# The last 512 output columns of each feed-forward computed block by block of tokens

## The chip, the core and the metric

One Trainium2 core out of eight runs the whole program. The metric is device microseconds of one execution; the times shown are the median of several. All data is fp32, the batch is 1, there are 512 tokens of width 1024.

## The reference, cut to what matters

The program is a first block (an mLSTM and pooling mixer and a mixture of 32 experts) followed by a second one of two layers. The change lies in the two feed-forwards of the second block and in the last norm:

```python
def rms_norm_2(x, g):
    xf = x.astype(jnp.float32)
    y = xf * lax.rsqrt(jnp.mean(xf * xf, axis=-1, keepdims=True) + EPS)
    return (y * g.astype(jnp.float32)).astype(x.dtype)

def swiglu(h, w_gu, w_down):
    gu = h @ w_gu
    g, u = jnp.split(gu, 2, axis=-1)
    return (jax.nn.silu(g) * u) @ w_down

def second_block(x, ...):
    k = v = None
    for l in range(DEPTH_2):            # 2 layers
        if l < N_A:                     # layer 0: gmlp
            x = x + gmlp_mixer(rms_norm_2(x, a_norm[l]), ...)
        else:                           # layer 1: attention
            k, v = shared_kv(x, kv_norm, kv_w)
            x = x + diff_attention(rms_norm_2(x, b_norm[j]), k, v, ...)
        x = x + swiglu(rms_norm_2(x, ffn_norm[l]), ffn_w_gu[l], ffn_w_down[l])
    return rms_norm_2(x, final_norm)
```

The hidden width of a feed-forward is 2816, that is 22 slices of 128.

## The kernel before

**Products.** Every fp32 factor is held as two fp32r parts, high and low, and a product is three matmuls (`mm3`: high x high, high x low, low x high), 128x128 stationary and 512 columns moving. The token matrix X stands in SBUF as four blocks (`tb`) of 128 tokens.

**The stream of weights.** `Stream` (W) holds all weights in the order of their use as items of at most 1 MB. SyncE loads each into a raw buffer. ScalarE makes the high part (`W.high`, L191, or L195 where a gain is multiplied in), VectorE the low part (`W.low`, L210, or L214 with a gain), each in two halves. There are four places for pairs of high and low parts (two early on, three within attention, of which the first `vv` item keeps one). An item's place may be written once the item that stood there before is released: `W.ends[before]`, for which ScalarE waits in `W.high`. `W.depth(j)` says how many items from j on have a predecessor in their place that is older than j. `W.high(e, j + W.depth(j))` and `W.low(...)` split up to there.

**The banks of sums.** `Ring` (R) plans the eight PSUM banks ahead: `R.claim` waits until a bank is free, `R.fill` tells that it is full, `R.free` that it has been read.

**A feed-forward** (`ffn_pe`, `ffn_act`, `ffn_vec`) runs over three groups of slices, 8, 8 and 6. In each group gate and up products (`fg`, `fu`) give the hidden values AT, and then the down products `fd{l}.{f0}.{h}` give half h (512 columns) of the output for all four blocks of tokens. Each half takes two weight items, of 4 and 4 slices, in the last group of 4 and 2. `n_pe` runs over the items outside and over the blocks inside: all four blocks with the first item, then all four with the second. The first item is released in the middle (`W.mid`, semaphore `w_used`), the second by the last full bank. `nd` counts the down items of a layer, 0, 2, ... 10; `nd == 10` is the last half of the last group, `fd{l}.16.1`.

VectorE adds each bank to X (`add_vec`, L845). For `fd{l}.16.1` it also calls `then`: one block behind the add it waits for ScalarE's sum of squares (`rms_act`, L689) and GpSimd's root (`rms_pool`, L694 and L696), then scales the rows. After feed-forward 0 the scaling is `normalize_vec` (L706), and `late_features_pe(e, 3)` transposes the rows (L731) into eight banks, of which ScalarE and VectorE make `hT4h` and `hT4l` (L761, L769). Behind that attention's products begin. `late_features_pe` also issues an unused product (`idle_pe`) ahead of block 0 and another ahead of slices 4 to 6. After feed-forward 1 the scaling is `last`, the output's norm (L260, `X<-X,small,GF`), and ScalarE issues the stores of the rows (L3075, L3077), each one block late.

**The order around the change**, in each engine's own queue. ScalarE: `W.high` for both items of the pair, then squares of blocks 0 to 3. VectorE: `W.low` for both items, then adds and `then`. The items that follow the last pair of layer 0 are two of `vv` (v weights), then `q`, `k`, `q`, ... Nothing follows the last pair of layer 1.

Of the kernel before, what the change touches and what calls it, by code (L numbers as in the profile page):

```python
# [11 lines left out]
ALU = mybir.AluOpType  # L12
# [3 lines left out]
P = 128  # L16
D = 1024
T = 512
TB = 4
# [213 lines left out]
def program(nc, g, out):  # L233
    ctx = ExitStack()
    with ctx:
# [19 lines left out]
        S = Sems(nc, ctx)  # L255
        R = Ring(S, [ctx.enter_context(nc.psum_tensor(f"ps{i}", [P, 512], F32)) for i in range(8)])
        W = Stream(S)

        def stt(e, o, x, s, y, o1, o2):
            return e.scalar_tensor_tensor(out=o, in0=x, scalar=s, in1=y, op0=o1, op1=o2)  # L260

        def mm(e, o, l, r, start, stop):
            return e.matmul(o, l, r, start=start, stop=stop, skip_group_check=True)  # L263

        def mm3(e, o, l, r, start, stop):
            mm(e, o, l[0], r[0], start, False)
            mm(e, o, l[0], r[1], False, False)
            return mm(e, o, l[1], r[0], False, stop)


        X = sb("X", [P, TB, D])
# [6 lines left out]
        small = sb("small", [P, 64])  # L278
        LASTG = sb("LASTG", [P, 4])
        LASTI = sb("LASTI", [P, 4], I32)  # L280
        GF = sb("GF", [P, D])
# [109 lines left out]
        AT = [sb("ATh", [P, 8, T], F32R), sb("ATl", [P, 8, T], F32R)]  # L391
# [101 lines left out]
        def n_plan(name, item, js, freed):  # L493
            for j in js[:-1]:
                W.mid(j)
            R.plan(name, TB, freed)
            W.ends[js[-1]] = R.full(name, TB - 1)

        A_, V_ = "bank_act", "bank_vec"
# [104 lines left out]
        def ffn_plan(l):  # L604
            R.plan(f"tf{2 if l == 0 else 4}", 8, V_)
            ng = nd = 0
            for f0, fn in FG:
                for f in range(0, fn, 2):
                    R.plan(f"fg{l}.{ng}", 2, A_)
                    W.ends[W.index[f"fg{l}"][ng]] = R.full(f"fg{l}.{ng}", 1)  # L610
                    R.plan(f"fu{l}.{ng}", 2, V_)
                    W.ends[W.index[f"fu{l}"][ng]] = R.full(f"fu{l}.{ng}", 1)
                    ng += 1
                for h in range(2):
                    n_plan(f"fd{l}.{f0}.{h}", "fd", W.index[f"fd{l}"][nd:nd + 2], V_)
                    nd += 2

        ffn_plan(0)
# [101 lines left out]
        def idle_pe(e, b, n):  # L720

            for _ in range(n):
                mm(e, b[:, :].rearrange("p (a n) -> p a n", a=4), ident[:, :], ident[:, :].unsqueeze(1).broadcast_to([P, 4, P]),
                   True, True)

        def late_features_pe(e, c):

            def turn(tb, kcs):
                for kc in kcs:
                    b = R.bank(f"tf{c}", kc)  # L730
                    i = e.transpose(b[:, tb * P:(tb + 1) * P], XN[:, tb, kc * P:(kc + 1) * P], ident[:, :])  # L731
                    if tb == TB - 1:
                        i.then_inc(*R.fill(f"tf{c}", kc))

            for kc in range(4):
                R.claim(e, f"tf{c}", kc)
            def rows(tb):
                return S("xn"), SECOND[tb] if c == 1 else 4 * norm_of[c] + tb + 1

            for tb in range(3):  # L740
                e.wait_ge(*rows(tb))
                if tb == 0:
                    idle_pe(e, R.bank(f"tf{c}", 0), 1)
                turn(tb, range(4))
            for kc in range(4, 7):
                R.claim(e, f"tf{c}", kc)
            idle_pe(e, R.bank(f"tf{c}", 4), 1)
            for tb in range(3):
                turn(tb, range(4, 7))
            e.wait_ge(*rows(3))  # L750
            turn(3, range(7))
            R.claim(e, f"tf{c}", 7)
            for tb in range(TB):
                turn(tb, [7])
# [82 lines left out]
                seen += kn  # L837
                k0 = (k0 + kn) % nk

        def add_vec(e, names, h, then=None):  # L840

            hs = slice(h * 512, (h + 1) * 512)
            for tb, name in enumerate(names):
                e.wait_ge(*R.full(*name))
                e.tensor_tensor(X[:, tb, hs], X[:, tb, hs], R.bank(*name)[:, :], ALU.add).then_inc(*R.free(*name))  # L845
                if then is not None and tb > 0:
                    then(tb - 1)
            if then is not None:
                then(TB - 1)


# [1566 lines left out]
        def ffn_pe(e, l, hT, AT, c):  # L2418
            late_features_pe(e, c)
            ng = nd = 0  # L2420
            for f0, fn in FG:
                for f in range(0, fn, 2):
                    for m in ("fg", "fu"):
                        t_pe(e, W.index[f"{m}{l}"][ng], [(f"{m}{l}.{ng}", 0), (f"{m}{l}.{ng}", 1)], hT,
                             (lambda kc: feature(e, c, kc)) if ng == 0 and m == "fg" else None, True)
                    ng += 1
                for h in range(2):
                    n_pe(e, W.index[f"fd{l}"][nd:nd + 2], f"fd{l}.{f0}.{h}", AT, 0, fn,
                         (lambda kc: e.wait_ge(S("a_lo"), 22 * l + f0 + kc + 1)) if h == 0 else None)
                    nd += 2  # L2430

        def ffn_act(e, own, l, hT, AT, c, norm, x_ready):
# [27 lines left out]
        def ffn_vec(e, own, l, hT, AT, c, then):  # L2460
            features_vec(e, c, hT, lambda kc: col("fn", 8 * l + kc))
            ng = nd = 0
            for f0, fn in FG:
                for f in range(0, fn, 2):
                    for m in ("fg", "fu"):
                        j = W.index[f"{m}{l}"][ng]
                        W.low(e, j + W.depth(j))
                    for k in range(2):
                        e.wait_ge(*R.done(f"fg{l}.{ng}", k))
                        e.wait_ge(*R.full(f"fu{l}.{ng}", k))  # L2470
                        e.tensor_tensor(tmpT[k][:, :], tmpT[k][:, :], R.bank(f"fu{l}.{ng}", k)[:, :], ALU.mult).then_inc(  # L2471
                            *R.free(f"fu{l}.{ng}", k))
                        e.wait_ge(S("a_hi"), 22 * l + f0 + f + k + 1)
                        e.tensor_tensor(AT[1][:, f + k, :], tmpT[k][:, :], AT[0][:, f + k, :].bitcast(F32),
                                        ALU.subtract).then_inc(S("a_lo"), 1)
                    ng += 1
                for h in range(2):
                    for j in W.index[f"fd{l}"][nd:nd + 2]:
                        W.low(e, j + W.depth(j))
                    add_vec(e, [(f"fd{l}.{f0}.{h}", tb) for tb in range(TB)], h, then if f0 + fn == 22 and h == 1 else None)  # L2480
                    nd += 2


# [573 lines left out]
        @block.scalar  # L3057
        def _(e):
            own = Own(S("act_self"))
            first_act(e, own)  # L3060
            experts_act(e, own)
            more_act(e)
            join_act(e, own)
            gmlp_act(e, own)
            ffn_act(e, own, 0, hT3, AT, 2, 4, lambda tb: R.done("go1", tb))
            attn_act(e, own)
            e.wait_ge(*R.done("as7", 7))
            e.dma_start(GF[:, :], g["final_norm_2"].partition_broadcast(P)).then_inc(S("fgb"), 16)
            ffn_act(e, own, 1, hT5, AT5, 4, 6, lambda tb: R.done(f"ao1.{tb}"))
            for tb in range(TB):  # L3070
                e.wait_ge(*R.done("fd1.16.1", tb))
                rms_act(e, 7, tb)
                if tb > 0:
                    e.wait_ge(S("x_last"), tb)
                    e.dma_start(out[0, (tb - 1) * P:tb * P, :], X[:, tb - 1, :]).then_inc(S("out"), 16)  # L3075
            e.wait_ge(S("x_last"), 4)
            e.dma_start(out[0, 3 * P:, :], X[:, 3, :]).then_inc(S("out"), 16)  # L3077
            e.wait_ge(S("out"), 64)

        @block.vector  # L3080
        def _(e):
            own = Own(S("vec_self"))
            first_vec(e, own)
            experts_vec(e, own)
            more_vec(e)
            join_vec(e, own)
            gmlp_vec(e, own)
            ffn_vec(e, own, 0, hT3, AT, 2, lambda tb: normalize_vec(e, 5, tb))
            attn_vec(e, own)

            def last(tb):
                e.wait_ge(S("rstd"), 4 * 7 + tb + 1)
                if tb == 0:
                    e.wait_ge(S("fgb"), 16)
                stt(e, X[:, tb, :], X[:, tb, :], small[:, 8 + tb:9 + tb], GF[:, :], ALU.mult, ALU.mult).then_inc(S("x_last"), 1)

            ffn_vec(e, own, 1, hT5, AT5, 4, last)

# [41 lines left out]
```

## Time and profile before

| | |
|---|---|
| median of 3 runs | 2085.39 us (2083.49 to 2088.24) |
| profiled execution | 2085.79 us |
| its span | 2084.0 us |
| mean granted TensorE clock | 0.983 of 2.4 GHz |
| TensorE busy | 1966.2 us, 94% |
| VectorE busy | 1188.4 us, 57% |
| ScalarE busy | 970.2 us, 47% |
| GpSimd busy | 186.4 us, 9% |

Busy time of TensorE counts matmuls whose ends are modelled. In the timelines each row begins with its start and its length in us, both from the span's start; a row with x2 or more merges neighbours of one kind. Brackets give the idle time of the engine before the row and what ended it.

### The profile page before, as it was taken

Reading aid. Unit: us, or ns where it says so; the run is one execution under the profiler, and the core shown is the slowest. Engines: PE = TensorE matmul, PEld = TensorE weight load, DVE = VectorE, ACT = ScalarE, POOL = GpSimd, SP = SyncE. Lnnn points to the kernel's source line nnn. Section 1 sums busy time; section 2 is a strip of 40 time slices with the busy share of each in tenths; the row PEclk is TensorE's granted clock in tenths of the full one; section 3 lists DMA queues with packets and bytes.
Section 4 is the critical chain, followed back from the end, with each engine's and each line's share of the span. In section 5 each row is a group of like instructions: output and inputs, shape, how many; then the busy total and the mean of one; then the engine's idle time right before and its main releaser. Section 6 shows DMA issues by size and latency. Waiting matters only on the chain.

```text
span 2084.0 us, 22887 instructions
## 1 busy us (share of the span) xinstructions
PE 1966.2 (94%) x8924; PEld 1572.5 (75%) x8924; DVE 1188.4 (57%) x1547; ACT 970.2 (47%) x1469; POOL 186.4 (9%) x250
## 2 busy tenths in 40 slices
PE   4989989999999999989999999998999989999997
PEld 3758767777777777758888888886777768888886
DVE  7776688888888888862543333324345343333322
ACT  3433268778878787744232222124445442222221
POOL 3100110121211110010000000001011100000000
PEclk8999999999999999999999999999999999999999
DMA  8464479999999999952323323222112123323211
GB/s 282 158 210 168 172 245 337 352 352 368 357 351 349 345 335 349 331 174 81 101 81 101 102 81 101 91 91 84 61 41 81 41 68 125 101 98 101 87 39 41
DMA packets 199832, 366.49 MB, mean 176 GB/s; under 512 B 13450, under 2 KB 83863, under 8 KB 199722
## 3 DMA queue, kind: packets, MB, share of 16 engines
q1 hardware_dynamic: 180960, 342.91, 47.6%
q10 hardware_dynamic: 8714, 11.46, 1.6%
q0 software_dynamic: 10048, 10.62, 1.5%
q8 instruction: 73, 1.20, 0.2%
q14 instruction: 37, 0.30, 0.0%
HBM read 365.05 MB, written 24.65 MB: 187 GB/s over the span
## 4 chain that ended last, share of the span: by engine, by line
PE 87%; DVE 7%; DMA 2%; issue 2%; ACT 1%; SPq 1%; POOL 0%; DVEq 0%; POOLq 0%; ACTq 0%
PE ps L263 85%; DVE wlo L210 2%; DMA raw<-in_w_in 1%; PE ps L2031 1%; DVE GM L2104 1%; SPq L886 1%; PE ps L731 1%; DMA raw<-in_ada_w 0%; DMA raw<-in_w_expert_down 0%; DVE acc L260 0%; PE ps L2608 0%; DVE hT5l L260 0%; DVE hT4l L769 0%; DVE X L845 0%; ACT XN L689 0%
## 5 line engine op out<-in xcount | busy, mean ns | idle before, releaser
L210 DVE TENSOR_TENSOR wlo<-raw,whi 128x1024 fp32r<-128x1024 f32 (+1 forms) x576 | 671.5, 1216 | 317.2 <-ACT whi L191 313.7
L191 ACT ACTIVATE whi<-raw 128x1024 fp32r<-128x1024 f32 (+1 forms) x576 | 573.0, 1047 | 232.8 <-PE ps L263 215.2
L263 PE MATMUL ps<-hT5h,whi 128*128 128x512 f32 x352 | 137.8, 391 | 6.3 <-DVE wlo L210 6.3
L263 PE MATMUL ps<-hT5l,whi 128*128 128x512 f32 x352 | 137.5, 391 | 0.0
L263 PE MATMUL ps<-hT3h,whi 128*128 128x512 f32 x352 | 137.0, 389 | 0.6 <-DVE hT3l L260 0.6
L263 PE MATMUL ps<-hT5h,wlo 128*128 128x512 f32 x352 | 137.4, 390 | 0.0
L263 PE MATMUL ps<-hT3l,whi 128*128 128x512 f32 x352 | 136.9, 389 | 0.0
L263 PE MATMUL ps<-hT3h,wlo 128*128 128x512 f32 x352 | 136.9, 389 | 0.0
L2471 DVE TENSOR_TENSOR tmpT<-tmpT,ps 128x512 f32<-128x512 f32 x44 | 30.1, 684 | 139.6 <-PE ps L263 139.6
L263 PE MATMUL ps<-whi,XT1h 128*128 128x512 f32 x256 | 102.1, 399 | 0.0
L263 PE MATMUL ps<-whi,XT0h 128*128 128x512 f32 x256 | 101.0, 395 | 1.1 <-DVE XT0l L2057 1.1
L263 PE MATMUL ps<-whi,XT1l 128*128 128x512 f32 x256 | 100.6, 393 | 0.0
L263 PE MATMUL ps<-wlo,XT1h 128*128 128x512 f32 x256 | 100.4, 392 | 0.0
L263 PE MATMUL ps<-whi,XT0l 128*128 128x512 f32 x256 | 99.8, 390 | 0.0
L263 PE MATMUL ps<-whi,GTh 128*128 128x512 f32 x256 | 99.7, 389 | 0.0
L263 PE MATMUL ps<-wlo,XT0h 128*128 128x512 f32 x256 | 99.7, 389 | 0.0
L263 PE MATMUL ps<-wlo,GTh 128*128 128x512 f32 x256 | 99.6, 389 | 0.0
L263 PE MATMUL ps<-whi,GTl 128*128 128x512 f32 x256 | 99.6, 389 | 0.0
L845 DVE TENSOR_TENSOR X<-X,ps 128x512 f32<-128x512 f32 x64 | 43.3, 686 | 92.4 <-PE ps L263 92.4
L694 POOL TENSOR_SCALAR small<-small 128x1 f32<-128x1 f32 x32 | 11.0, 342 | 946.5 <-ACT XN L689 888.4
L2446 ACT ACTIVATE tmpT<-ps 128x512 f32<-128x512 f32 x44 | 26.4, 600 | 134.7 <-PE ps L263 132.9
L263 PEld LDWEIGHTS ps<-hT5h,whi 128*128 128x128 f32 x352 | 66.5, 189 | 20.4 <-issue 6.5
(446 smaller groups left out, 4062.5 us busy)
## 6 DMA issues: line engine op xcount, KB each, us to landing
raw<-in_w_expert_gate SPq DMA_DIRECT2D x64, 1024.0 KB, 8.2
raw<-in_w_expert_up SPq DMA_DIRECT2D x64, 1024.0 KB, 8.0
raw<-in_w_expert_down SPq DMA_DIRECT2D x64, 1024.0 KB, 6.7
raw<-in_ffn_w_gu SPq DMA_DIRECT2D x44, 1024.0 KB, 5.0
raw<-in_ffn_w_down SPq DMA_DIRECT2D x20, 1024.0 KB, 5.0
raw<-in_ada_w SPq DMA_DIRECT2D x24, 512.0 KB, 5.4
raw<-in_w_in SPq DMA_DIRECT2D x8, 1024.0 KB, 5.7
raw<-in_a_w_in SPq DMA_DIRECT2D x8, 1024.0 KB, 9.3
```

The costliest lines, as they stand in the source:

```text
L191: e.activation(hi[:, c], raw[:, c], ACT.Copy).then_inc(self.S("w_hi"), 1)
L210: e.tensor_tensor(lo[:, c], raw[:, c], hi[:, c].bitcast(F32), ALU.subtract).then_inc(self.S("w_lo"), 1)
L263: return e.matmul(o, l, r, start=start, stop=stop, skip_group_check=True)
L694: e.tensor_scalar(out_, x, EPS, None, ALU.add).then_inc(*own.up())
L731: i = e.transpose(b[:, tb * P:(tb + 1) * P], XN[:, tb, kc * P:(kc + 1) * P], ident[:, :])
L845: e.tensor_tensor(X[:, tb, hs], X[:, tb, hs], R.bank(*name)[:, :], ALU.add).then_inc(*R.free(*name))
L886: e.dma_start(EARLY[n].rearrange("p (c n) -> p c n", c=2), ada_w[:, 2 * c:2 * c + 2, j * D:(j + 1) * D]).then_inc(S(f"early{n}"), 16)
L2031: i = e.transpose(b[:, k * P:(k + 1) * P], GM[:, k * P:(k + 1) * P], ident[:, :])
L2104: e.tensor_tensor(GM[:, :], SG[n % 2][:, :], R.bank(f"eu{n}")[:, :], ALU.mult).then_inc(*R.free(f"eu{n}"))
L2446: e.activation(tmpT[k][:, :], R.bank(f"fg{l}.{ng}", k)[:, :], ACT.Silu).then_inc(*R.free(f"fg{l}.{ng}", k))
L2471: e.tensor_tensor(tmpT[k][:, :], tmpT[k][:, :], R.bank(f"fu{l}.{ng}", k)[:, :], ALU.mult).then_inc(*R.free(f"fu{l}.{ng}", k))
```

## The change

The last down half of each feed-forward (`nd == 10`) is computed by a new function `blocks_pe`, which has the blocks of tokens outside and both items inside. The middle release of the pair's first item is gone: both items are released by the last block's full bank. `add_vec` gets a parameter `apart`; with it `then(tb)` is called right behind add tb. The feed-forwards pass it, the other callers don't. The first unused product of `late_features_pe` is left out for attention (`c == 3`). The last block of output rows is scaled and stored in two halves of 512 columns, and the stores of the other blocks are issued right behind their own square.

```diff
@@ ffn_plan
                 for h in range(2):
-                    n_plan(f"fd{l}.{f0}.{h}", "fd", W.index[f"fd{l}"][nd:nd + 2], V_)
+                    js = W.index[f"fd{l}"][nd:nd + 2]
+                    if nd < 10:
+                        n_plan(f"fd{l}.{f0}.{h}", "fd", js, V_)
+                    else:
+
+                        R.plan(f"fd{l}.{f0}.{h}", TB, V_)
+                        for j in js:
+                            W.ends[j] = R.full(f"fd{l}.{f0}.{h}", TB - 1)
                     nd += 2
@@ late_features_pe
+        APART = (3,)
...
-                if tb == 0:
+                if tb == 0 and c not in APART:
                     idle_pe(e, R.bank(f"tf{c}", 0), 1)
@@
-        def add_vec(e, names, h, then=None):
+        def blocks_pe(e, js, name, hT):
+
+            for tb in range(TB):
+                b = R.claim(e, name, tb)
+                kc, nk = 0, sum(W.w[j][1] for j in js)
+                for j in js:
+                    kn = W.w[j][1]
+                    for k in range(kn):
+                        if tb == 0 and 2 * k % kn == 0:
+                            e.wait_ge(*W.half(j, 2 * k // kn))
+                        i = mm3(e, b[:, :], [x[:, kc, tb * P:(tb + 1) * P] for x in hT], [x[:, k, :] for x in W.parts(j)],
+                                kc == 0, kc == nk - 1)
+                        kc += 1
+                i.then_inc(*R.fill(name, tb))
+
+        def add_vec(e, names, h, then=None, apart=False):
...
-                if then is not None and tb > 0:
+                if then is not None and apart:
+                    then(tb)
+                elif then is not None and tb > 0:
                     then(tb - 1)
-            if then is not None:
+            if then is not None and not apart:
                 then(TB - 1)
@@ ffn_pe
-                    n_pe(e, W.index[f"fd{l}"][nd:nd + 2], f"fd{l}.{f0}.{h}", AT, 0, fn,
-                         (lambda kc: e.wait_ge(S("a_lo"), 22 * l + f0 + kc + 1)) if h == 0 else None)
+                    if nd < 10:
+                        n_pe(e, W.index[f"fd{l}"][nd:nd + 2], f"fd{l}.{f0}.{h}", AT, 0, fn,
+                             (lambda kc: e.wait_ge(S("a_lo"), 22 * l + f0 + kc + 1)) if h == 0 else None)
+                    else:
+                        blocks_pe(e, W.index[f"fd{l}"][nd:nd + 2], f"fd{l}.{f0}.{h}", AT)
@@ ffn_vec
-                    add_vec(e, [(f"fd{l}.{f0}.{h}", tb) for tb in range(TB)], h, then if f0 + fn == 22 and h == 1 else None)
+                    add_vec(e, [(f"fd{l}.{f0}.{h}", tb) for tb in range(TB)], h, then if f0 + fn == 22 and h == 1 else None, True)
@@ ScalarE, end
-                if tb > 0:
-                    e.wait_ge(S("x_last"), tb)
-                    e.dma_start(out[0, (tb - 1) * P:tb * P, :], X[:, tb - 1, :]).then_inc(S("out"), 16)
-            e.wait_ge(S("x_last"), 4)
-            e.dma_start(out[0, 3 * P:, :], X[:, 3, :]).then_inc(S("out"), 16)
-            e.wait_ge(S("out"), 64)
+                if tb < TB - 1:
+                    e.wait_ge(S("x_last"), tb + 1)
+                    e.dma_start(out[0, tb * P:(tb + 1) * P, :], X[:, tb, :]).then_inc(S("out"), 16)
+            for h in range(2):
+                e.wait_ge(S("x_last"), TB + h)
+                e.dma_start(out[0, 3 * P:, h * 512:(h + 1) * 512], X[:, 3, h * 512:(h + 1) * 512]).then_inc(S("out"), 16)
+            e.wait_ge(S("out"), 16 * (TB + 1))
@@ VectorE, last(tb)
-                stt(e, X[:, tb, :], X[:, tb, :], small[:, 8 + tb:9 + tb], GF[:, :], ALU.mult, ALU.mult).then_inc(S("x_last"), 1)
+                for h in range(1 if tb < TB - 1 else 2):
+                    hs = slice(0, D) if tb < TB - 1 else slice(h * 512, (h + 1) * 512)
+                    stt(e, X[:, tb, hs], X[:, tb, hs], small[:, 8 + tb:9 + tb], GF[:, hs], ALU.mult, ALU.mult).then_inc(S("x_last"), 1)
```

## Rows read from the trace of the kernel before

**Rows 1.** The page: the span, and the chain that ended last, by engine.

```profile
span 2084.0 us, 22887 instructions
...
PE 87%; DVE 7%; DMA 2%; issue 2%; ACT 1%; SPq 1%; POOL 0%; DVEq 0%; POOLq 0%; ACTq 0%
```

**Rows 2.** Timeline of TensorE, 1427 to 1446 us, end of feed-forward 0.

```profile
1427.99 0.39 PE L263 MATMUL ps<-whi,ATl 128*128 128x512 f32 x1
...
1431.73 2.05 PE L263 MATMUL ps<-ident 128*128 128x512 f32 x2 [3.35 <-DVE XN L706]
1433.57 2.25 PE L731 MATMUL ps<-ident,XN 128*128 128x128 f32 x12
...
1436.52 2.35 PE L731 MATMUL ps<-ident,XN 128*128 128x128 f32 x20
1443.37 0.80 PE L263 MATMUL ps<-whi,hT4h 128*128 128x512 f32 x1 [4.51 <-DVE hT4l L769]
```

**Rows 3.** Windows: length, busy PE, PEld, DVE, ACT, POOL, then clock, DMA share, GB/s.

```profile
1412.00:1428.40 16.40, 16.38 (x73) 13.23 (x71) 7.59 (x16) 5.88 (x12) 0.00 (x0) 1.00 0.39 127
...
1443.30:1448.30 5.00, 4.93 (x12) 3.91 (x13) 3.40 (x15) 3.39 (x9) 0.00 (x0) 0.50 0.01 2
1448.30:1450.30 2.00, 2.00 (x10) 1.63 (x9) 1.20 (x4) 0.00 (x0) 0.71 (x1) 0.92 0.03 7
```

**Rows 4.** Timeline of ScalarE, 1370 to 1440 us.

```profile
1412.16 2.56 ACT L195 ACTIVATE whi<-raw,VT 128x512 fp32r<-128x512 f32 x4 [2.87 <-PE ps L263]
1423.04 3.31 ACT L195 ACTIVATE whi<-raw,VT 128x256 fp32r<-128x256 f32 x8 [8.31 <-PE ps L263]
...
1437.81 2.56 ACT L761 ACTIVATE hT4h<-ps 128x512 fp32r<-128x512 f32 x5 [2.93 <-PE ps L731]
```

**Rows 5.** Timeline of VectorE, 1370 to 1440 us.

```profile
1399.15 1.29 DVE L210 TENSOR_TENSOR wlo<-raw,whi 128x512 fp32r<-128x512 f32 x2
...
1424.78 3.28 DVE L214 SCALAR_TENSOR_TENSOR wlo<-raw,VT,whi 128x256 fp32r<-128x256 f32 x8 [8.51 <-ACT whi L195]
1427.97 1.28 DVE L845 TENSOR_TENSOR X<-X,ps 128x512 f32<-128x512 f32 x2
1430.83 0.75 DVE L706 TENSOR_SCALAR XN<-X,small 128x1024 f32<-128x1024 f32 x1 [1.58 <-POOL small L696]
1431.50 0.68 DVE L845 TENSOR_TENSOR X<-X,ps 128x512 f32<-128x512 f32 x1
...
1435.87 0.75 DVE L706 TENSOR_SCALAR XN<-X,small 128x1024 f32<-128x1024 f32 x1 [0.76 <-POOL small L696]
```

**Rows 6.** Timeline of GpSimd, 2053 to 2084 us.

```profile
2071.60 0.91 POOL L694 TENSOR_SCALAR small<-small 128x1 f32<-128x1 f32 x1 [0.49 <-ACT XN L689]
...
2074.30 0.26 POOL L694 TENSOR_SCALAR small<-small 128x1 f32<-128x1 f32 x1 [1.14 <-ACT XN L689]
```

**Rows 7.** Timeline of VectorE, 2053 to 2084 us, end of feed-forward 1.

```profile
2068.28 0.69 DVE L845 TENSOR_TENSOR X<-X,ps 128x512 f32<-128x512 f32 x1 [11.55 <-PE ps L263]
2069.64 0.69 DVE L845 TENSOR_TENSOR X<-X,ps 128x512 f32<-128x512 f32 x1 [0.67 <-PE ps L263]
2071.15 1.28 DVE L260 SCALAR_TENSOR_TENSOR X<-X,small,GF 128x1024 f32<-128x1024 f32 x1 [0.82 <-POOL small L696]
2072.35 0.68 DVE L845 TENSOR_TENSOR X<-X,ps 128x512 f32<-128x512 f32 x1
...
2077.29 1.28 DVE L260 SCALAR_TENSOR_TENSOR X<-X,small,GF 128x1024 f32<-128x1024 f32 x1 [0.76 <-POOL small L696]
```

**Rows 8.** Timeline of ScalarE, 2053 to 2084 us: issues of the output's stores.

```profile
2072.47 0.36 ACTq L3075 DMA_DIRECT2D out_x<-X  x1
...
2078.61 0.34 ACTq L3077 DMA_DIRECT2D out_x<-X  x1
```

**Rows 9.** Windows (columns as in rows 3): bytes of the last store.

```profile
2079.50:2080.00 0.50, 0.00 (x0) 0.00 (x0) 0.00 (x0) 0.00 (x0) 0.00 (x0) 0.50 1.00 410
```

**Rows 10.** Groups of VectorE by form, 1000 to 2084 us: a 128x512 scaling.

```profile
L260 DVE SCALAR_TENSOR_TENSOR widehi<-widelo,ST,widehi 128x512 f32<-128x512 f32 x4 | 3.0, 748 | 0.0
```

## The prediction

> **What bounds the kernel now.** I read the page first. TensorE is the engine of the chain that ended last for most of the span [rows 1], so an edit away from TensorE counts only where TensorE stands still for it. The change touches two such places, the ends of the two feed-forwards, so I read each engine's timeline there, and the windows for the clock and the matmul rate.
>
> End of feed-forward 0, the hand-over to attention. I call the end of the last matmul of `fd0.16.1` T3: the row starts at 1427.99 and is 0.39 long, so T3 = 1428.38 [rows 2]. TensorE runs without a gap up to there, 73 matmuls in the stretch of 16.4 us [rows 3]; six products take 1.36 us (the two adds released by TensorE in rows 7 are one block of six apart), so one takes 0.2267 us. The pair has 72 products, 16.32 us, and so began at 1412.06. What the reader is to see next is what stands **ahead** of the adds in VectorE's queue: eight 128x256 pieces of `wlo` with the gain column VT, from 1424.78, and only then two adds at 1427.97 [rows 5]. The 128x256 form is a query-weight item, the first of `q`. Its high parts are made by ScalarE from 1423.04, and that group was released by TensorE [rows 4]. In the code it is the place reuse: `W.high(e, j + W.depth(j))` and `W.low(...)` with j the second weight of the pair reach three items beyond it, and with four places the third goes into the place of the pair's **first** weight. That place comes free by `W.mid` after 4 blocks x 4 slices x 3 = 48 matmuls: 1412.06 + 48 x 0.2267 = 1422.94, and the split starts 0.10 later. The item ahead of it likewise started at 1412.16, 0.10 after the end of the pair before. So the release is what it waits for, to 0.1 us.
>
> After T3 the rows are normalized, the last from 1435.87 to 1436.62 [rows 5]; TensorE transposes, ScalarE makes `hT4h` from 1437.81 [rows 4], and TensorE's next matmul of the attention starts at 1443.37 [rows 2]. From T3 to there TensorE does little else than wait.
>
> End of feed-forward 1, the end of the kernel. No weight is left to split: VectorE had been idle for 11.55 us before the first add at 2068.28. The adds are released by TensorE 1.36 us apart, so the last block is full at T3' = 2068.28 + 3 x 1.36 = 2072.36. The last scaling of rows starts at 2077.29 and takes 1.28 [rows 7], and its store is issued at 2078.61 [rows 8].
>
> **The change, part by part.**
>
> (1) TensorE's work. The same 72 products per pair with other order; no row gives a reason for another rate, and both weights are ready early: the second weight's low parts are 128x512 pieces at 1399.15 [rows 5], 13 us before the pair starts, where block 0 will now want them 12 products (2.7 us) in. T3 and T3' stay: 0. If cover were missing it would be a late split, and there is none.
>
> (2) Feed-forward 0, the release moves. `n_plan`'s mid release goes; both weights are now released by the last block. The query item's split therefore starts at T3 + 0.10 = 1428.48 instead of 1423.04: 5.44 later. And it is queued, on ScalarE and on VectorE, ahead of the squares and ahead of all four adds. So although blocks 0 to 2 are complete 12.2, 8.2 and 4.1 us before T3, nobody adds them. VectorE's first piece starts 1.74 after ScalarE's first (1423.04 to 1424.78), the first add 3.19 after that (1427.97): the first add comes at 1428.48 + 1.74 + 3.19 = 1433.41.
>
> (3) Feed-forward 0, "rows scaled as they come". `add_vec` now calls `then(tb)` right behind add tb, not one block later. VectorE's queue is in order, so behind each add it waits for ScalarE's square and GpSimd's root of those rows, and the next add waits behind it. An add to its own normalization is 1427.97 to 1430.83 = 2.86; a normalization to the next add is 1430.83 to 1431.50 = 0.67 [rows 5]. A turn is 3.53. Normalizations start at 1436.27, 1439.80, 1443.33 and 1446.86, the last ends at 1447.61: 10.99 later than 1436.62. Where blocks arrive 4.08 us apart (18 products) a turn of 3.53 would be free; here all four are ready, so the turns add up.
>
> (4) TensorE behind it. It turns blocks 0 to 2 while it waits, but the two idle products and nine transposes (slices 4 to 6) come after block 2's rows, at 1444.08. At the pace of 1431.73 to 1433.78 for the idle pair (2.05) and 2.25 for twelve transposes [rows 2]: 0.14 + 4 x 0.19 + 2.05 + 9 x 0.19 = 4.66, so 1448.74, then the first transpose of block 3, 0.2, and `hT4h` at 1448.95. That is 11.14 after 1437.81. At the faster pace it is ready for block 3 before 1447.61 and `hT4h` starts at 1447.9: 10.1. I take 11.1, since TensorE has been mostly idle by then. From `hT4h` to the first matmul is VectorE's eight subtractions, 5.56 (1437.81 to 1443.37), unchanged. Removing the idle product at block 0 for attention is worth 0: it would run while block 1's rows are still out.
>
> (5) The clock at the restart. The granted clock is 0.50 (the 1.2 GHz level) from 1443.3 to 1448.3 with 12 matmuls where full speed does 22, and 0.92 behind it [rows 3]. TensorE had been idle 4.51 us [rows 2]. Twelve matmuls at 0.427 instead of 0.2267 cost 2.4 us, paid now. After the change the gap ahead of the restart is some 3.5 us (transposes to about 1451, restart at 1454.5), with little work before: I take the same cost, 0, between -2.4 (restart at full speed) and +1.2 (six more slow matmuls). The Trainium skill, TensorE: Matmul & The Clock Gate, Part 1, says that an idle TensorE is stepped down to 1.2 GHz and returns only after sustained work; by it the longer stall gives no cheaper restart, and the sum stays as it is. The trace agrees in that the stretch behind the gap has clock 0.50.
>
> (6) Nothing later is starved: the load queue's next issues hang on low parts 5.4 us later than before, and what they load is three or four items ahead. 0, and with 11 us more of stall ahead of it no less time for them than now.
>
> Feed-forward 0: +11.1 (10.1 to 11.6 without the clock, 7.7 to 12.8 with it).
>
> (7) Feed-forward 1, the adds. Nothing is queued ahead of them. Blocks are complete at 2060.1, 2064.2, 2068.3 and 2072.36. A turn is add to scaling 2068.28 to 2071.15 = 2.87, scaling to next add 2071.15 to 2072.35 = 1.20 [rows 7]: 4.07 against 4.08 of matmuls, just hidden. On ScalarE the store's issue (0.36, [rows 8]) now stands ahead of the next square: 2.87 + 1.28 + 0.04 + 0.36 = 4.55 after the add, the square is wanted 4.08 + 0.73 = 4.81 after it. It fits with 0.26 to spare. GpSimd's first step took 0.91 beside a running VectorE scaling and 0.26 without [rows 6]; in the new order VectorE waits while GpSimd works, so they no longer meet. The Trainium skill, SBUF — State Buffer, section "SBUF: two separate sides", has VectorE with two SBUF inputs and GpSimd exclude each other on a shared port pair. If they still met, a turn would be 0.65 longer and three turns would put the last add some 1.9 late; the order of instructions speaks against it.
>
> (8) The last rows. Add at 2072.36, first half from 2075.23. A 128x512 scaling is 0.75 [rows 10] and the next starts some 0.66 later, so the halves end at 2075.98 and 2076.64; the stores are issued at 2076.02 and 2076.68, the second 1.93 before 2078.61. The bytes of the last 512 KB run at 410 GB/s from about 2079.5 [rows 9], 1.28 us; the half has 0.64, and the first half is through by then. So the end moves by -1.93 - 0.64 = -2.57; if a store's time did not shrink with its size, -1.9; if turns also slipped, -0.5. I take -2.5.
>
> **Sum.** +11.1 - 2.5 = +8.6. The profiled execution took 2085.79 with a span of 2084.0: it would be 2094.4. It is 0.4 above the median 2085.39, which gives 2094.0.
>
> **The rivals.**
> - A, it gets faster: the split does not stand behind the blocks, because its place is free earlier. It decides from the point where the split's low parts are done before block 0 is (1416.14). Then the turns of 3.53 hide under 4.08, the last add is at 1428.40, its normalization ends at 1432.01, 4.6 before 1436.62, and with -2.5 the time is 2078.3. For it: blocks 0 to 2 are early. Against: the split starts 0.1 us behind the release, twice [rows 4]. 0.04.
> - B, no difference: only the moved release is paid, 5.4, since ScalarE and GpSimd work on several blocks together when four are ready. +5.4 - 2.5 = +2.9, 2088.3. Against: `then(tb)` stands in VectorE's own queue ahead of the next add. 0.05.
> - C, the restart keeps the full clock: 11.1 - 2.4 - 2.5 = +6.2, 2091.6. For it: the gap is an us shorter. Against: the long stall before. 0.13.
> - D, the restart is dearer or the tail gives less: +11.1 + 1.2 - 0.5 = +11.8, 2097.2. For it: margins of 0.01 and 0.26 us in (7). 0.13.
> - The forecast: 0.65, itself within about 2092.5 to 2095.5.
>
> **How the numbers follow.** C and D and the noise of a median (the runs shown span 4.75 us) give the range 2090 to 2098. A measurement tells 0.2%, 4.2 us, from no change. Slower by more: forecast, C and D, 0.91. Within: B, 0.05. Faster: A, 0.04.
>
> **What would show it.** In the trace after: the 128x256 pieces of `whi` start right behind the last matmul of feed-forward 0, the first X add about 5.4 us later than now, four adds 3.5 us apart, TensorE's gap from T3 to attention's first matmul near 26 us instead of 15. At the end: four adds about 4.1 us apart, the last at its block's end, two stores 0.66 apart, and the time from TensorE's last matmul to the span's end about 9.1 instead of 11.7. Adds of feed-forward 0 that start before T3 would make me wrong on the sign; adds closer than 3 us would mean B; a granted clock of 1.00 at the restart would mean C.

## The result, and the profile after

The changed kernel takes 2095.98 us (median of 6 runs, 2092.40 to 2096.81) against 2086.65 us of the kernel before (6 runs, 2083.49 to 2088.24). The ratio is 1.0043, with a 95% interval of 1.0031 to 1.0056: 9.3 us slower. The profiled execution took 2096.80 us with a span of 2095.0 us.

The chain of waits of the changed kernel, 1411 to 1462 us (start, length, what), shows the new order at the end of feed-forward 0.

```profile
1430.94 1.71 ACT whi L195 x4
...
1432.68 3.27 DVE wlo L214 x8
1435.94 0.61 DVE X L869
...
1449.38 2.05 PE ps L740 x10
...
1451.46 0.61 ACT hT4h L770
```

The high and the low parts of the query item stand between TensorE's last matmul and the first add; before, they lay beside the matmuls [rows 4, 5]. TensorE's timeline of the changed kernel, which answers to [rows 2]:

```profile
1430.45 0.39 PE L263 MATMUL ps<-whi,ATl 128*128 128x512 f32 x1
1439.61 1.09 PE L740 MATMUL ps<-ident,XN 128*128 128x128 f32 x4 [8.77 <-DVE XN L713]
1443.04 1.12 PE L740 MATMUL ps<-ident,XN 128*128 128x128 f32 x4 [2.34 <-DVE XN L713]
1446.57 1.11 PE L740 MATMUL ps<-ident,XN 128*128 128x128 f32 x4 [2.41 <-DVE XN L713]
1447.47 1.91 PE L263 MATMUL ps<-ident 128*128 128x512 f32 x2
1449.18 3.33 PE L740 MATMUL ps<-ident,XN 128*128 128x128 f32 x20
1457.02 0.79 PE L263 MATMUL ps<-whi,hT4h 128*128 128x512 f32 x1 [4.50 <-DVE hT4l L778]
```

From the end of the last matmul of feed-forward 0 (1430.45 + 0.39 = 1430.84) to attention's first (1457.02) are 26.18 us, where 14.99 were [rows 2]. I call this stretch the hand-over. The bursts of four transposes are 3.5 us apart: one turn of VectorE each. A turn is an add, the wait for the root of those rows, and their scaling, as VectorE's timeline of the changed kernel shows:

```profile
1435.86 0.68 DVE L869 TENSOR_TENSOR X<-X,ps 128x512 f32<-128x512 f32 x1
1438.71 0.75 DVE L713 TENSOR_SCALAR XN<-X,small 128x1024 f32<-128x1024 f32 x1 [2.17 <-POOL small L703]
1439.38 0.68 DVE L869 TENSOR_TENSOR X<-X,ps 128x512 f32<-128x512 f32 x1
```

VectorE's timeline at the end of the kernel, which answers to [rows 7]:

```profile
2085.45 0.69 DVE L869 TENSOR_TENSOR X<-X,ps 128x512 f32<-128x512 f32 x1
2088.30 1.41 DVE L260 SCALAR_TENSOR_TENSOR X<-X,small,GF 128x512 f32<-128x512 f32 x2 [2.17 <-POOL small L703]
```

The last block is added at 2085.45, as it fills, and 9.55 us later the span ends. Before, the last block was full at 2072.36 and the span ended 11.64 us later. I call this the tail.

The span grew by 11.0 us. The hand-over has 11.2 of them, the tail gives 2.1 back, attention and feed-forward 1 between them are 0.6 shorter (628.43 against 628.99), and the remaining 2.5 lie ahead of the change: the last matmul of feed-forward 0 ended at 1430.84 instead of 1428.38. Further profiles of the same code show what that part is. The kernel before reached this point at 1424.15 in one more execution and the changed one at 1429.28, and the other versions, which share all the code up to the last down half of feed-forward 0, lie between 1425.25 and 1430.38. So this part is no effect of the change, and the comparison below goes by stages, and not by spans:

| kernel | hand-over us | attention and feed-forward 1 us | tail us | ratio to before, 95% interval |
|---|---|---|---|---|
| before | 14.99 | 628.99 | 11.64 | |
| before, again | 16.26 | 623.55 | 11.64 | |
| changed | 26.18 | 628.43 | 9.55 | 1.0043, 1.0031 to 1.0056 |
| changed, again | 25.88 | 628.07 | 9.57 | |
| ffn1_only | 15.08 | 626.16 | 9.56 | 1.0001, 0.9990 to 1.0013 |
| apart_only | 20.84 | 629.02 | 9.61 | 1.0021, 1.0007 to 1.0036 |
| lagged | 22.53 | 628.23 | 9.62 | 1.0036, 1.0023 to 1.0048 |
| lagged_no_idle | 21.04 | 626.08 | 9.60 | 1.0013, 0.9997 to 1.0028 |
| no_idle | 25.19 | 628.38 | 9.58 | 1.0051, 1.0034 to 1.0067 |
| late_old_order | 11.34 | 626.12 | 9.64 | 0.9980, 0.9969 to 0.9990 |
| split_late | 9.63 | 623.27 | 9.64 | 0.9952, 0.9934 to 0.9970 |
| late_whole | 9.63 | 623.45 | 9.55 | 0.9964, 0.9945 to 0.9982 |
| late_no_idle | 9.63 | 623.82 | 9.57 | 0.9967, 0.9954 to 0.9980 |

Hand-over: end of the last matmul on AT to the start of the first on `hT4h`. The middle runs from there to the last add of feed-forward 1 (for the two kernels of the old order, to the time when the last block is full, three steps of 1.36 us behind the first add). Tail: from there to the end of the span. Each ratio is against runs of the kernel before taken alongside; one execution of `late_whole` (4439 us) and one of before (5067 us), each over twice as long as the rest, are left out.

### The profile page after: what moved, and what is told of

Its sections match the earlier page's. It is cut to its first block, busy times and chain, and to the rows that moved or that the text cites. A ratio compares the mean times of both kernels' runs of the same rounds, so it can differ in the third digit from the quotient of the medians.

```text
span 2095.0 us, 22885 instructions
## 1 busy us (share of the span) xinstructions
PE 1975.6 (94%) x8922; PEld 1579.5 (75%) x8922; DVE 1188.5 (57%) x1548; ACT 970.3 (46%) x1469; POOL 187.0 (9%) x250
## 4 chain that ended last, share of the span: by engine, by line
PE 88%; DVE 6%; DMA 2%; issue 2%; ACT 1%; SPq 1%; POOL 0%; DVEq 0%; POOLq 0%; ACTq 0%
PE ps L263 85%; DVE wlo L210 2%; DMA raw<-in_w_in 1%; PE ps L2057 1%; DVE GM L2130 1%; DMA raw<-in_w_expert_down 1%; SPq L912 1%; PE ps L740 1%; DMA raw<-in_ada_w 0%; ACT XN L696 0%; DVE acc L260 0%; PE ps L2637 0%; DVE hT5l L260 0%; DVE X L869 0%; DVE hT4l L778 0%
```

## Experiments

**Where the split is queued.** `split_late` is the change with one bound more, on both engines:

```diff
                     for j in W.index[f"fd{l}"][nd:nd + 2]:
-                        W.high(e, j + W.depth(j))
+                        W.high(e, min(j + W.depth(j), W.index["q"][0] if l == 0 else len(W.w)))
...
                     for j in W.index[f"fd{l}"][nd:nd + 2]:
-                        W.low(e, j + W.depth(j))
+                        W.low(e, min(j + W.depth(j), W.index["q"][0] if l == 0 else len(W.w)))
```

Attention's own `take("k", 0)` then splits both the query and the key item, behind the features.

> The change as it is, but in feed-forward 0 the splits run only up to the first query item, which is split behind attention's features instead of ahead of the adds. My theory (the query item's split, queued ahead of the adds, is what turns the change into a loss): adds of feed-forward 0 come 4.08 us apart and start before TensorE's last matmul; from that matmul's end to attention's first matmul 9.5 us (26.2 in the changed kernel, 15.0 before), so 16.7 us less than the changed kernel and 7.6 less than before (with the 2.1 gained at the end): ratio to before 0.996, about 2079. Rival (block-wise order or the one-by-one scaling costs by itself, whatever is queued): the stretch stays above 20 us and the kernel at or above before.

VectorE's timeline of `split_late`, 1400 to 1450 us:

```profile
1418.32 0.75 DVE L713 TENSOR_SCALAR XN<-X,small 128x1024 f32<-128x1024 f32 x1 [2.17 <-POOL small L703]
1419.54 0.69 DVE L869 TENSOR_TENSOR X<-X,ps 128x512 f32<-128x512 f32 x1 [0.46 <-PE ps L263]
...
1427.70 0.69 DVE L869 TENSOR_TENSOR X<-X,ps 128x512 f32<-128x512 f32 x1 [0.47 <-PE ps L263]
1430.55 0.75 DVE L713 TENSOR_SCALAR XN<-X,small 128x1024 f32<-128x1024 f32 x1 [2.17 <-POOL small L703]
...
1439.82 6.42 DVE L214 SCALAR_TENSOR_TENSOR wlo<-raw,VT,whi 128x256 fp32r<-128x256 f32 x16 [1.26 <-ACT whi L195]
```

The adds are released by TensorE, 4.08 us apart, and three blocks are scaled before the last matmul ends at 1427.66. The hand-over is 9.63 us. The split now comes at 1439.82 as 16 pieces, beside attention's first products, which hide it: VectorE is through with it at 1446.24, and TensorE, without a gap, reaches the first product with a query weight at 1460.56. The time is 2072.39 us, ratio 0.9952: faster than both kernels. The rival falls. Of the 10 to 11 us below before, the two stages account for 7.4 (5.36 in the hand-over, 2.0 in the tail), and the interval of the ratio still holds that (it would be 0.9964). The middle stage is dealt with below.

**The end of the kernel alone.** `ffn1_only` leaves feed-forward 0 as before:

```diff
-                    if nd < 10:
+                    if nd < 10 or l == 0:
...
-... then if f0 + fn == 22 and h == 1 else None, True)
+... then if f0 + fn == 22 and h == 1 else None, l == 1)
...
-        APART = (3,)
+        APART = ()
```

> Feed-forward 0 and its hand-over as before, feed-forward 1 and the stores as in the change. My theory: the end gives 2.1 us (last add to span's end 9.55 instead of 11.64 from the last block's end), nothing else moves: ratio 0.999, 2084.5. Rival (the loss sits in the shared code or in feed-forward 1 too): at or above before.

The tail is 9.56, 2.1 less than before, and the hand-over 15.08 as before. The ratio of 1.0001 (0.9990 to 1.0013) holds the expected 0.9990 only at its edge: by the time this gain can't be told from nothing, by the stage it is there in every profile.

**The two halves of the loss.** `lagged` is the change with the scaling of feed-forward 0 one block behind the add again (`l == 1` in place of `True` in `add_vec`'s call). `apart_only` is the change with feed-forward 0 in the old order of products (`nd < 10 or l == 0`), so that the middle release is kept, and the scaling right behind each add. Both leave out the first unused product of attention's transposes, as the change does.

> The change, but in feed-forward 0 the scaling is again called one block behind the add; the query item's split still stands ahead of the adds. My theory (loss of 11.1 = 5.44 from the later release + 5.55 from turns that add up): only 5.4 of the 11.2 are left, from last matmul to attention's first 20.4 us, 5.7 less than the changed kernel, 3.3 above before: ratio 1.0016, 2090. Rival (the late release alone carries the loss): stays at 26 us.

> The change, but feed-forward 0 computes its last half in the old order (both weights outside, middle release kept); scaling is called right behind each add. My theory: first add as before, 0.4 ahead of the last matmul's end, then turns of 3.53: last matmul to attention's first 20.5 us, 5.6 above before; with the end's gain 3.5 above before, ratio 1.0017. Rival (turns cost nothing): 15 us, ratio 0.999.

`apart_only`: 20.84, 5.85 above before, 5.6 expected. The serial turns make up 5.51 of them: the last rows are ready 13.75 us after the last matmul (1441.18), before 8.24. The other 0.34 lie between the rows and the start of the features. `lagged`: 22.53 instead of 20.4, and the ratio is 1.0036 instead of 1.0016, which its interval of 1.0023 to 1.0048 doesn't hold. The last rows were ready when expected (scaling from 1442.82, 0.75 long, 13.65 after the last matmul), yet the features began 3.33 us later, where before it was 1.19. TensorE's timeline of `lagged` shows with what it was busy:

```profile
1442.12 1.12 PE L740 MATMUL ps<-ident,XN 128*128 128x128 f32 x4 [0.89 <-DVE XN L713]
1443.03 1.91 PE L263 MATMUL ps<-ident 128*128 128x512 f32 x2
1444.73 3.22 PE L740 MATMUL ps<-ident,XN 128*128 128x128 f32 x20
```

So `lagged` lies 7.54 above before: the rows come 5.41 later, and 2.14 more lie between them and the features. The two halves, 7.54 and 5.85, are together more than the 11.19 of the changed kernel, because TensorE's own work behind the rows counts in full only in `lagged`: in the changed kernel the rows come 10.95 later, and the features only 0.24 more.

**The unused product.** `no_idle` and `lagged_no_idle` are the change and `lagged` without it in attention's transposes:

```diff
-            idle_pe(e, R.bank(f"tf{c}", 4), 1)
+            if c not in APART:
+                idle_pe(e, R.bank(f"tf{c}", 4), 1)
```

> The changed kernel without the unused product ahead of slices 4 to 6 in attention's transposes (1.71 us there, at the low clock). My theory (after block 2's rows TensorE's own work at the low clock, not block 3's rows, sets the start of the features): without it the nine transposes end before block 3's rows are there, so last matmul of feed-forward 0 to attention's first goes from 26.2 to 25.0 us. Rival (block 3's rows set it): stays at 26.2.

> The kernel with the lagged scaling in feed-forward 0, and without the unused product ahead of slices 4 to 6. With that product, last matmul to attention's first was 22.5 us where 20.4 were expected: block 3's rows were ready 13.65 us after the last matmul as expected, but the features began only 3.33 us behind their start-of-scaling plus 0.75. My theory: TensorE's idle product (1.7 us) and nine transposes at the low clock stand between block 2's rows and block 3's transposes; without the product the stretch is 20.8 us. Rival (block 3's rows or the banks set it): stays at 22.5.

25.19 against 26.18 (25.0 expected), and 21.04 against 22.53 (20.8 expected). In `no_idle` TensorE waits 0.48 us for block 3's rows, in the changed kernel it doesn't. So there TensorE itself, working at the slow pace, sets the start of the features. The times can't show this us: `no_idle` has 1.0051, the changed kernel 1.0043. What no run shows is whether the first unused product, which all four of these versions leave out, would have brought TensorE to the faster pace; step (4) put its removal at 0. The same edit on top of the late split:

> The late split without the unused product ahead of slices 4 to 6. Block 3's rows set the start of the features here (TensorE waited 0.55 us for them), so my theory says nothing changes: last matmul to attention's first 9.6 us, same time as the late split within 1 us; the product's 0.9 us would cost only if it kept the clock up, in which case the restart gets dearer. Ratio to before 0.996. Rival (the product delays the features): 8.8 us.

9.63, as with the product: TensorE waits 1.41 us for the rows there, with the product 0.55. Its time (2076.73, ratio 0.9967) is not better. Whether it is within 1 us of the late split's can't be told from two sets of runs with intervals of about 3 us to either side.

**What the block order is worth.** `late_old_order` has the late split, but feed-forward 0 in the old order with lagged scaling and with the first unused product of attention's transposes.

> Late split, but feed-forward 0 in the old order with the scaling one block behind; feed-forward 1 as in the change. It tells what the block order itself is worth at attention's hand-over. Blocks then fill 1.36 us apart: last block's rows normalized about 4.5 to 5.1 us after the last matmul instead of 3.65, attention's first matmul 11.4 us after it (9.63 with the block order, 15.0 before). My theory: 1.8 us above the late split in this stretch, the other 3.6 of its 5.4 come from moving the split. Rival (block order carries the gain): 15 us.

The hand-over is 11.34. From 14.99 the late split alone takes 3.65, and the block order, with the scaling right behind each add, then 1.71 more. (Against the second profile of before, 16.26, the late split takes 4.92.) Most of what feed-forward 0 had to give lay in the queue, not in the order of the products.

**The two stores.** `late_whole` is `split_late` with the last block scaled by one instruction and stored whole.

> The version with the late split, but the last block of output rows is scaled and stored whole, not in halves. In the changed kernel the second half's store is issued 4.30 us after the last add of feed-forward 1, and 5.25 us later the span ends; before, 5.39 us after the issue of the whole store. My theory now: the whole store is issued 4.18 us after the last add, so last add to span's end is 9.57 us, the same as the 9.55 to 9.64 of the halved versions: halving is worth nothing, all of the end's gain comes from the block order. Rival (the predicted one: half the bytes, 0.64 us less): 10.1 us or more.

The tail is 9.55 (9.57 expected), where the versions with halves have 9.55 to 9.64. DMA issues with the size and the time to landing, of the changed kernel from 2085 us:

```profile
out_x<-X ACTq DMA_DIRECT2D x1, 512.0 KB, 2.6
out_x<-X ACTq DMA_DIRECT2D x2, 256.0 KB, 2.1
```

A half does land in 0.5 us less, but its issue is 0.13 later than the whole store's (4.30 against 4.17 behind the last add), and the span ends about 3.1 us after the landing instead of 2.8. Why the end takes longer after two stores was not tried. The whole gain of the tail, 2.1 us, is there without the halves. It comes from the block order together with the scaling and storing right behind each block, which no run takes apart: before, the last scaling began 4.93 us after the last block was full (2072.36 to 2077.29), now 2.85 (2085.45 to 2088.30).

**The clock within attention.** `split_late` was 5.7 us shorter in the middle stage than the profile of before, in code that is the same but for the place of one split and the order of feed-forward 1's last down half.

> The kernel before, unchanged: another profiled execution, for the granted clock within attention. The late split's attention (from its first matmul on 623.3 us to the last add) was 5.7 us shorter than before's (629.0), with three dips of the clock fewer. If the dips come and go from run to run, this profile shows another number of them than before's four; if they belong to the kernel, the same ones.

> The changed kernel again, for another profile. Last matmul of feed-forward 0 to attention's first 26.2 us and last add to span's end 9.6 us as in the first profile; attention (first matmul to the last add of feed-forward 1) between 623 and 629 us, by how many dips of the granted clock this execution has.

The kernel before, again, took 623.55 us there, 5.4 less than its first profile, and the changed kernel, again, 628.07. The window from 80 to 100 us behind attention's first matmul, in the first profile of before and then in the second (length, busy PE, PEld, DVE, ACT, POOL, granted clock, DMA share, GB/s):

```profile
1523.40:1543.40 20.00, 17.05 (x75) 11.82 (x74) 6.76 (x25) 9.69 (x26) 2.39 (x3) 0.83 0.17 53
```

```profile
1520.40:1540.40 20.00, 17.05 (x93) 12.83 (x92) 9.10 (x28) 11.27 (x36) 3.98 (x5) 1.00 0.18 54
```

TensorE is idle for 2.95 us in this window in both profiles, in one piece. In one the clock falls for part of it (0.83) and 75 matmuls are recorded, in the other it stays and 93 are. The same gap, 2.94 or 2.95 us, stands there in all thirteen profiles, and the middle column of the table goes with the clock of this window: 0.83 in the six profiles with 628.07 to 629.02, 0.91 in the three with 626.08 to 626.16, 1.00 in the four with 623.27 to 623.82. The kernel before is in the first group and in the last, so an unchanged kernel makes a difference of 5.4 us by itself. The dips come and go: the second profile lacks this one and the one 180 to 200 us behind attention's first matmul (0.91 in the first profile, 1.00 in the second). But all three versions with both the late split and the block order are in the last group, with one profile each. That an edit makes the dips rarer is not shown, and not excluded. The times don't speak for it: the ratios of `late_whole` and `late_no_idle` are, to 0.0003, what hand-over and tail alone give (0.9964).

## Why the prediction was right

It said 2094.0 with a range of 2090 to 2098, slower with 0.91. Measured: 2095.98, 9.3 us slower, where 8.6 were forecast.

- **The release, step (2).** Expected: the split 0.10 behind the last matmul, VectorE's pieces 1.74 and the first add 4.93 behind the split's start. Measured: 1430.84 to 1430.94, 1432.68 and 1435.86, that is 0.10, 1.74 and 4.92. `split_late` shows that the split's place ahead of the adds is what makes the adds late.
- **The turns, step (3).** Expected 3.53 each. Measured: the adds of blocks 0 to 3 at 1435.86, 1439.38, 1442.90 and 1446.43, 3.52 each. The last rows were ready 10.95 later than before, 10.99 expected. `apart_only`, without the late release, has 5.51 from the turns and 5.85 in all.
- **TensorE behind it, step (4).** The features start 20.62 after the last matmul, 11.19 more than the 9.43 of before; 11.14 were expected from the slow pace. `no_idle` confirms that TensorE's own work ends last there. The same mechanism is why a single part can't be undone for its full price: `lagged` won 3.65 and not 5.7. The expectation of `lagged` left TensorE's own work out.
- **The clock at the restart, step (5).** No change was expected. The restart was slow again: attention's first ten matmuls start some 0.43 us apart and the following ones 0.23, where before it was the first twelve. That is 0.4 us, and it lies in the middle stage. The gap ahead of it was 4.50 us and not the 3.5 expected: TensorE's last transposes end 1.05 us behind the start of the features (1452.51 and 1451.46), as they did before (1438.87 and 1437.81), so the rows of before already gave 4.5. With that, rival C's reason, a gap shorter by an us, had no ground. C did not come in the profile; in the second profile of the changed kernel the first two or three matmuls ran at the full rate, and the seven behind them at the slow one.
- **Nothing later is starved, step (6).** The middle stage was 628.43 against 628.99.
- **Feed-forward 1, step (7).** Turns of 4.08 (2077.29, 2081.37, 2085.45) against 4.08 of matmuls, the last add not late (2085.45, the last matmul's end is at 2085.41). GpSimd's first step was 0.22 in all four blocks, no longer 0.91.
- **The last rows, step (8): the term that was mis-sized.** -2.5 was taken, -2.1 measured. The part from the earlier issue was right: 4.30 us behind the full block instead of 6.25, which is -1.95. The further -0.64, half the bytes, came to -0.1 in the changed kernel and to nothing against `late_whole`: a half lands 0.5 us sooner, but the span's end doesn't follow it.
- **Rivals.** A: its mechanism was refuted for the changed kernel, but its condition, the split out of the way, is what `split_late` makes true. Its forecast of 4.6 less in the hand-over was 5.36, and with the tail's 2.0 the stages give 7.4, where A said 7.1. B would have had adds closer together than 3.5 us; they weren't. D did not come: the restart was no dearer, and the tail gave 2.1 and not 0.5.

The sum by stages is +11.19 - 2.09 = +9.1, beside the 9.3 of the medians. Part of its closeness is luck: in the second profile of before the hand-over was 16.26 us, since the transposes ran at the slow clock there too (the second unused pair took 1.83 us, in the first profile 1.02), and against that profile the hand-over grew by 9.9 us only (9.6 from second profile to second). That is just below the low end of step (4), 10.1. And the other gaps, 2.5 us ahead of the change and 0.6 in the middle, are of the size that two executions of one kernel differ by.

## What to carry to other kernels

When a change moves a release to a later point, look up what waits for it and what stands **behind** that wait in the same in-order queue: here the split of a weight that attention needs only behind its first 96 matmuls held up four adds that were wanted at once. Work done "as it comes" is only free while blocks arrive further apart than a turn takes; if they pile up behind a wait, the turns add up. Once prefetch, here the query item's split, is queued behind the urgent work, the same change goes from 9.3 us slower to some 7 to 10 us faster by the ratios of three versions; the stages account for about 7 of them.

## What the hardware showed that I had not expected

- Gaps of the same length in TensorE's work lower the granted clock in one execution and not in another: one window with 2.95 us idle had 0.83 and 1.00 in two profiles of the same kernel. The middle stage, which goes with this window's clock in all thirteen profiles, differed by 5.4 us between the two.
- Splitting the last store made each part land 0.5 us sooner (2.1 against 2.6) and the program end no sooner (9.55 to 9.64 us after the last add with halves, 9.55 with one store).
- The restart behind the hand-over, too, differs from one execution to the next. In the second profile of the changed kernel attention's first two matmuls took 0.50 and 0.39 us, in the first profile 0.79 and 0.63. TensorE's timeline of the second profile:

```profile
1455.16 0.50 PE L263 MATMUL ps<-whi,hT4h 128*128 128x512 f32 x1 [4.50 <-DVE hT4l L778]
1455.50 0.39 PE L263 MATMUL ps<-wlo,hT4h 128*128 128x512 f32 x1
...
1456.47 0.63 PE L263 MATMUL ps<-wlo,hT4h 128*128 128x512 f32 x1
```

Both times TensorE had idled 4.50 us, after working without a gap for 5.66 us (1445.00 to 1450.66) and 5.94. The full rate held for two or three matmuls, then the second profile was at the slow rate too. `lagged` did the same (0.50 and 0.40 us, after 5.83 us of work and the same 4.50). Why the clock came down later in one than in the other is open.
